# Gates in the output copies, adding gathers and a gate matmul for the last expert, in a two-layer mixture-of-experts step

## The chip, the cores and the metric

One core of a Trainium2 chip runs the whole kernel. The metric is the device time of one execution in microseconds (us), lower is better.

## The reference

One inference step of a decoder with two layers, for 512 prompt rows and 64 sample rows, 1024 columns, all in 32-bit floats. Each layer has a mixer, a residual with layer norm, a mixture of experts and a second residual with layer norm. The change touches the mixture and the norm behind it:

```python
for e in range(N_EXPERTS):                 # 16 experts, D_EXPERT = 256
    he = jax.nn.silu(h @ w_gate[e]) * (h @ w_up[e])
    y = y + gates[:, e:e + 1] * (he @ w_down[e])
x = layernorm(ALPHA * x + y)
```

`gates` has two nonzero entries in each row: the router picks a group of four experts and the two best inside it, and their two scores are normalised to the sum 1. So each row needs two experts only.

## The kernel before

The 576 rows are five tiles, four of 128 and one of 64 (`ROWS`, `NT` = 5). Each engine has its own program; the lines named here are those of the kernel before.

**Jobs and banks.** Each result of TensorE is a numbered job, and job n lives in bank n modulo 8 of the accumulation memory. `claim` waits until the job eight earlier is emptied, `take` waits for the result, `give` marks it emptied, `landed` waits until given jobs are emptied. The numbers are reserved for a version that runs every expert on all rows (288 jobs a layer, used when an expert has more than 128 rows). The usual version (`own_tokens`, line 1195) needs six jobs an expert: T0 and T1 (rows transposed), GU (hidden, 512 columns), HT (hidden transposed), D0 and D1 (the two halves of the output). At its end VectorE increments the semaphores for all the jobs that were left out (lines 2258 to 2265).

**The mixture.** When the router has assigned each row a slot of 128 for each of its two experts, GpSimd scatters the rows into the array `xrows` in main memory (ten indirect transfers, line 983), ScalarE loads 128 rows for each expert (line 1811), and TensorE goes through the experts. In step e it transposes the rows of expert e + 1 (line 1202), transposes the hidden activations of expert e - 1 (line 1222), computes the hidden layer of e (line 1212, 16 passes) and then the output of e - 1 (line 1232, 8 passes). ScalarE copies T0, HT and D0, computes the activation of GU (line 1830); VectorE copies T1 and D1 (line 2257) and computes the product of GU (line 2251). GpSimd stores the copied outputs, 128 rows of 4 KB for each expert, into `yrows` (line 992). SyncE loads the weights of the experts, 3 MB each, into eleven buffers as they come free (lines 958 to 961).

**The end of the mixture.** When all sixteen stores have landed, GpSimd gathers for each tile two rows for each row (ten indirect transfers into `yg`, line 998). VectorE multiplies each by its gate and adds it to `acc`, which ScalarE has filled with ALPHA times x (`combine`, line 2267, two operations at line 2271), then computes the statistics (`row_stats`, 2062: lines 2065, 2067, 2068). ScalarE takes the square root (`norm`, line 1777), VectorE inverts it and makes the offset (`scale_rows`, 2074 and 2075), ScalarE scales the rows (line 1779), VectorE multiplies and adds the norm's parameters (`affine`, 2082 and 2083). The order on VectorE is: scale of tile t, combine and statistics of tile t + 1, affine of tile t.

**Behind it.** After layer 1 each finished tile is stored by GpSimd and the kernel ends. After layer 0 the next mixer begins (`odd`): TensorE transposes each finished tile (`turn_x`, line 1139) and, from the second tile on, computes the latent projection of the tile before (line 1332, 16 passes of 416 columns, one bank). ScalarE's order there is norm of tile t + 1, copy of the transposed tile t (line 1772), copy of the latent projection of tile t - 1 (line 1871). The jobs in order are xT0 (two), xT1 (two), dtok0, xT2 (two), dtok1, and so on; they follow the 288 jobs of the layer. SyncE begins to load the weights of that mixer once all gathers have landed (line 963).

**The start of the kernel.** GpSimd clears `xrows` with one transfer (line 1066) and then stores parts of the pooling state: `pool_p` and `pool_s` in pieces of 60 bytes (512 and 4096 of them), `sgu` in rows. VectorE waits for these three stores before the first mixture.

## Time and profile before

| | |
|---|---|
| Median of 3 runs | 1265.58 us (1265.21 to 1266.97) |
| The profiled execution's own time | 1265.74 us |
| Its span | 1263.9 us |
| Busy TensorE matmul, VectorE, ScalarE, GpSimd | 86%, 41%, 24%, 9% of the span |
| Mixture of layer 0, first row transposes to last output | 228.4 to 414.9 us |
| Mixture of layer 1, the same | 1018.3 to 1204.1 us |

Times in rows are microseconds from the start of the span unless marked ns. PE is TensorE, PEld its weight load, DVE VectorE, ACT ScalarE, POOL GpSimd, SP SyncE. A matmul of 32-bit floats appears as two passes. In the chain of waits each row is the piece of work that released the next one; in the timeline the bracket gives the idle time before an instruction and what ended it.

### The profile page before, as it was taken

The page shows a single profiled execution, that of the slowest core. Times are in us where ns is not written, and L with a number is a line of the kernel's source. Part 1 is how long each engine was busy: PE and PEld are TensorE (multiplying, and loading weights), DVE is VectorE, ACT ScalarE, POOL GpSimd, SP SyncE. Part 2 cuts the span into 40 slices and gives each one's busy share as a digit, 9 for nine tenths or more (in the row PEclk, how much of TensorE's full clock was granted, in tenths as well). Part 3 has the DMA queues.
Part 4 walks back from the last instruction along what each step waited for, and adds up shares of the span by engine and source line. Part 5 has one row for each costly group of instructions (what it writes and reads, how often), then busy time and mean ns, then how long its engine had stood idle before and what let it go on. Part 6 is the DMA issues. An engine that isn't in the chain of part 4 may idle for free.

```text
span 1263.9 us, 19022 instructions
## 1 busy us (share of the span) xinstructions
PE 1089.5 (86%) x7162; PEld 667.3 (53%) x7162; DVE 517.6 (41%) x1330; ACT 302.9 (24%) x691; POOL 112.5 (9%) x152
## 2 busy tenths in 40 slices
PE   7999994799999189999899998999999379999910
PEld 3686452444444056777788875555554244444400
DVE  2570345111111553488545556666334511111155
ACT  0102123111111222323334331455312211111111
POOL 0010003000000300000211111210000300000030
PEclk9999996799999689999999997999999689999965
DMA  9568009899992632132322242854500989999251
GB/s 355 199 244 157 1 5 357 321 364 359 377 352 110 222 128 100 34 100 76 91 74 74 74 133 76 318 191 156 200 34 18 356 314 375 361 367 353 103 199 66
DMA packets 85380, 246.28 MB, mean 195 GB/s; under 512 B 9488, under 2 KB 50496, under 8 KB 66720
## 3 DMA queue, kind: packets, MB, share of 16 engines
q1 hardware_dynamic: 63584, 150.53, 33.9%
q0 software_dynamic: 17088, 77.64, 16.7%
q10 hardware_dynamic: 4608, 16.78, 3.4%
q8 instruction: 62, 1.02, 0.3%
q14 instruction: 38, 0.31, 0.1%
HBM read 205.63 MB, written 58.16 MB: 209 GB/s over the span
## 4 chain that ended last, share of the span: by engine, by line
PE 83%; DVE 8%; issue 4%; DMA 3%; ACT 1%; POOL 1%; POOLq 0%; DVEq 0%; SPq 0%; ACTq 0%
PE bank L1212 18%; PE bank L1148 10%; PE bank L1232 9%; PE bank L1358 8%; PE bank L1282 5%; PE bank L1455 4%; PE bank L1300 3%; PE bank L1202 2%; PE bank L1332 2%; DVE acc L2271 2%; DVE stat L2065 1%; PE bank L1708 1%; PE bank L1733 1%; PE bank L1162 1%; PE bank L1139 1%
## 5 line engine op out<-in xcount | busy, mean ns | idle before, releaser
L1148 PE MATMUL bank<-ring,cat 128*128 128x512 f32 (+1 forms) x320 | 141.0, 594 | 1.3 <-ACT cat L1851 1.3
L1212 PE MATMUL bank<-ring,work 128*128 128x512 f32 x256 | 114.7, 600 | 0.0
L1358 PE MATMUL bank<-xT,ring 128*128 128x288 f32 x448 | 110.9, 407 | 0.0
L2251 DVE TENSOR_TENSOR work<-work,bank 128x256 f32<-128x256 f32 x32 | 13.5, 421 | 219.5 <-ACT work L1830 219.5
L1358 PEld LDWEIGHTS bank<-xT,ring 128*128 128x128 f32 x448 | 84.6, 190 | 24.1 <-issue 1.5
L1148 PEld LDWEIGHTS bank<-ring,cat 128*128 128x128 f32 (+1 forms) x320 | 56.0, 179 | 74.0 <-issue 73.9
L1212 PEld LDWEIGHTS bank<-ring,work 128*128 128x128 f32 x256 | 48.3, 194 | 54.7 <-issue 54.7
L1282 PE MATMUL bank<-xT,ring 128*128 128x288 f32 x256 | 63.1, 407 | 0.0
L1830 ACT ACTIVATE work<-bank 128x256 f32<-128x256 f32 x32 | 12.3, 384 | 208.3 <-PE bank L1212 208.3
L1202 PE MATMUL bank<-const,work 128*128 128x128 f32 x256 | 36.4, 291 | 29.3 <-DMA work<-xrows 29.3
L1232 PE MATMUL bank<-ring,work 128*128 128x512 f32 x128 | 57.7, 593 | 1.0 <-issue 1.0
L2257 DVE COPY work<-bank 128x512 f32<-128x512 f32 x32 | 22.1, 692 | 87.3 <-PE bank L1232 87.3
L1202 PEld LDWEIGHTS bank<-const,work 128*128 128x128 f32 x256 | 32.8, 151 | 44.3 <-DMA work<-xrows 29.6
L1282 PEld LDWEIGHTS bank<-xT,ring 128*128 128x128 f32 x256 | 48.3, 190 | 13.9 <-issue 0.8
L1139 PE MATMUL bank<-const,x 128*128 128x128 f32 (+1 forms) x120 | 17.6, 299 | 38.5 <-DVE x L2083 38.5
L992 POOL DMA_DIRECT2D yrows<-work x32 | 17.2, 538 | 373.9 <-DVE work L2257 370.1
L2090 DVE SCALAR_TENSOR_TENSOR acc<-x,bank 128x512 f32<-128x512 f32 (+1 forms) x20 | 13.7, 685 | 76.3 <-PE bank L1148 76.3
L1300 PE MATMUL bank<-ring,xT 128*128 128x512 f32 (+1 forms) x80 | 37.1, 626 | 7.7 <-DMA ring<-in_stream_dram 7.7
L1212 PE MATMUL bank<-work 128*128 128x512 f32 x96 | 42.5, 592 | 0.0
L1232 PEld LDWEIGHTS bank<-ring,work 128*128 128x128 f32 x128 | 24.2, 190 | 31.1 <-issue 31.1
L1139 PEld LDWEIGHTS bank<-const,x 128*128 128x128 f32 (+1 forms) x120 | 14.6, 163 | 45.7 <-DVE x L2083 41.5
L1820 ACT COPY work<-bank 128x512 f32<-128x512 f32 x32 | 18.7, 586 | 77.7 <-PE bank L1202 77.6
(426 smaller groups left out, 1865.7 us busy)
## 6 DMA issues: line engine op xcount, KB each, us to landing
ring<-in_stream_dram SPq DMA_DIRECT2D x71, 1024.0 KB, 7.4
cat<-in_stream_dram SPq DMA_DIRECT2D x16, 1024.0 KB, 9.0
work<-xrows ACTq DMA_DIRECT2D x32, 512.0 KB, 5.6
xT<-in_stream_dram SPq DMA_DIRECT2D x16, 1024.0 KB, 9.0
work<-in_stream_dram SPq DMA_DIRECT2D x16, 1024.0 KB, 10.5
yrows<-work POOLq DMA_DIRECT2D x32, 512.0 KB, 9.2
by_batch<-in_pages_dram SPq DMA_DIRECT2D x128, 128.0 KB, 2.4
xrows<-work POOLq DMA_DIRECT2D x1, 8192.0 KB, 27.4
```

Of the source, the lines that this page charges most:

```text
L1139: i = pe.transpose(bank(n, 4, P)[:, k, 0:r], x[0:r, tile, P * (4 * g + k):P * (4 * g + k + 1)], ident[0:r, 0:r])
L1148: i = pe.matmul(bank(n)[0:ROWS[tile], :], cat[:, k, tok(tile)], slot(w[k // 4], 4, 512)[:, k % 4, :], start=(k == 0), stop=(k == KC - 1))
L1202: i = pe.transpose(bank(n, 4, P)[:, k, :], xg[:, e % NXG, P * (4 * g + k):P * (4 * g + k + 1)], ident)
L1212: i = pe.matmul(bank(n), xgT[:, e % 2, k, :], sparse_slot(layer, 3 * e + k // 4, 4, 512)[:, k % 4, :], start=(k == 0), stop=(k == KC - 1))
L1232: i = pe.matmul(bank(n), hTS[:, e % 2, k, :], sparse_slot(layer, 3 * e + 2, 2, D_MODEL)[:, k, 512 * half:512 * half + 512], start=(k == 0) ...
L1282: i = pe.matmul(bank(n)[:, 0:nn], slot(w, KC, 256)[:, k, P * (m % 2):P * (m % 2) + P], xT[:, k, a:a + nn], start=(k == 0), stop=(k == KC - 1))
L1300: i = pe.matmul(bank(n)[0:ROWS[tile], :], xT[:, k, tok(tile)], slot(w, 4, 512)[:, k % 4, :], start=(k == 0), stop=(k == KC - 1))
L1332: i = pe.matmul(bank(n)[0:ROWS[tile], 0:D_COLS], xT[:, k, tok(tile)], slot(w[k // 4], 4, 512)[:, k % 4, 0:D_COLS], start=(k == 0), stop=(k ...
L1358: i = pe.matmul(bank(n + s)[:, 0:nn], slot(w, KC, 256)[:, k, P * (m % 2):P * (m % 2) + P], xT[:, k, a:a + nn], start=(k == 0), stop=(k == ...
L1455: i = pe.matmul(bank(n, 4, HD)[rc, j, :], d[a][rc, half, j, :], d[b][rc, half, j, :], start=True, stop=True)
L2257: give(dve.tensor_copy(yS[:, (e - 1) % NYS, 512:], bank(n)), n)
L2271: dve.scalar_tensor_tensor(acc[0:r, tile, :], yg[0:r, tile, k, :], gate2[0:r, tile, k:k + 1], acc[0:r, tile, :], ALU.mult, ALU.add).then_i ...
```

## The change

- `yrows` is stored, already multiplied by the gates. For that each row's two gates are scattered into a new array `grows` (ten indirect transfers of 4 bytes a row, behind the row scatters on GpSimd's queue), and one transfer loads them back as a column for each expert (`gate_of`). ScalarE and VectorE apply them while they copy D0 and D1.
- The gathers write into `acc` and add to it. The second gather of a tile waits for its first; the order is 0, 1, 2, 3 (first rows), 0 (second), 4, then 1, 2, 3, 4 (second).
- The last expert is neither stored nor gathered. Its region of `yrows` is cleared at the start of the kernel. VectorE builds for each tile a matrix with the gate of each row in the column of its slot (`gate_at`), TensorE transposes the five matrices in step 1 (jobs G0 and G1), ScalarE copies the whole last output, and TensorE multiplies the transposed gates with it, two halves a tile, in the last ten of the 288 jobs. VectorE adds these to `acc` after the tile's gathers (`add_last`).
- In step 15 TensorE computes the output of expert 14 before the hidden layer of expert 15, and the copies follow.
- The semaphores of the jobs left out are incremented by SyncE instead of VectorE, and SyncE waits for three tiles' gathers instead of five.
- VectorE's order at the end is: scale of tile t, `add_last` of tile t + 1, affine of tile t, statistics of tile t + 1.
- In `odd` the square root of tile t + 1 comes before the copy of the transposed tile t on ScalarE, the row scaling of tile t + 1 after it.

```diff
@@ -70,7 +70,7 @@
...
 put("ident", np.eye(P))
-put("lane", i % D_ROPE * 1.0)
+put("lastslots", np.tile((N_EXP - 1) * P + np.arange(P) * 1.0, (P, 1)))
 put("cum", np.concatenate([chunk & (i <= t), chunk & (i < t)], 1))
@@ -282,18 +282,28 @@
-SPARSE = ["T0", "T1", "GU", "HT", "D0", "D1"]
+LAST_E = N_EXP - 1
 SPARSE_ORDER = {}
...
 for e in range(N_EXP + 1):
-    for at, kind in ((e + 1, "T0"), (e + 1, "T1"), (e - 1, "HT"), (e, "GU"), (e - 1, "D0"), (e - 1, "D1")):
+    steps = [(e + 1, "T0"), (e + 1, "T1")] + ([(LAST_E, "G0"), (LAST_E, "G1")] if e == 1 else []) + [(e - 1, "HT")]
+    outputs = [(e - 1, "D0"), (e - 1, "D1")]
+    for at, kind in steps + (outputs + [(e, "GU")] if e == LAST_E else [(e, "GU")] + outputs):
         if 0 <= at < N_EXP:
             SPARSE_ORDER[at, kind] = len(SPARSE_ORDER)
+DENSE = N_EXP * (8 + 2 * NT)
 def sparse_job(layer, e, kind):
     return job(f"{layer}.e0") + SPARSE_ORDER[e, kind]
+def last_job_of(layer, tile, half):
+    return job(f"{layer}.e0") + DENSE - 2 * NT + 2 * tile + half
 def rec(name, tile, half=0):
@@ -551,13 +561,15 @@
+last_gates = sem("last_gates")
+gates_scattered = sem("gates_scattered")
+gates_loaded = sem("gates_loaded")
-combined = [sem(f"combined{k}") for k in range(LAYERS)]
@@ -742,10 +753,15 @@
...
 spare = [t[:, SLOT * i:SLOT * i + SLOT] for t in (cat_t, xT_t, work) for i in range(2)]
+tail_t = sb("tail", P + NS)
+gate_at = [view(cat_t, 4 * D_MODEL + P * tile, P) for tile in range(NT - 1)] + [view(tail_t, 0, P)]
+gate_by = [view(work, 4 * D_MODEL + P * tile, P) for tile in range(NT - 1)] + [view(tail_t, P, NS)]
 zero = work[:, WORK - D_MODEL - 16:WORK - 16]
...
 xrows = nc.dram_tensor("xrows", [(N_EXP - 1) * P + P * NT, D_MODEL], F32).ap()
+grows = nc.dram_tensor("grows", [(N_EXP - 1) * P + P * NT, 1], F32).ap()
+gate_of = view(stat, 400, N_EXP)
 yrows = nc.dram_tensor("yrows", [N_EXP * P, D_MODEL], F32).ap()
@@ -959,7 +975,17 @@
...
     load_spare(layer, j)
-for tile in range(NT):
+first = job(f"{layer}.e0")
+used = len(SPARSE_ORDER)
+landed(sp, first + used - NBANK, NBANK)
+for b in range(NBANK):
+    skipped = sum(1 for m in range(first + used, first + DENSE - 2 * NT) if m % NBANK == b)
+    sp.sem_inc(filled[b], skipped)
+    sp.sem_inc(emptied[b], skipped)
+at = FIRST_EXPERT_BLOCK[layer]
+for i in range(NSLOT):
+    sp.sem_inc(slot_loaded[i], 16 * sum(1 for j in range(NSLOT, 3 * N_EXP) if (at + j) % NSLOT == i))
+for tile in range(3):
     sp.wait_ge(gathered[layer][tile], 32)
@@ -973,7 +999,7 @@
...
 def pool_mixture(layer):
-    pool.wait_ge(rows_cleared, 16)
+    pool.wait_ge(rows_cleared, 48)
     pool.wait_ge(early_rows, layer + 1)
@@ -983,22 +1009,39 @@
...
                 in_=x[0:r, tile, :], in_offset=None).then_inc(scattered[layer], 16)
+    for tile in range(NT):
+        r = ROWS[tile]
+        for k in range(2):
+            pool.indirect_dma_start(
+                out=grows, out_offset=bass.IndirectOffsetOnAxis(ap=rowi[0:r, 2 * tile + k:2 * tile + k + 1], axis=0),
+                in_=gate2[0:r, tile, k:k + 1], in_offset=None).then_inc(gates_scattered, 16)
     flag = is_crowded(pool, layer)
...
     with pool.Else():
-        for e in range(N_EXP):
+        pool.wait_ge(gates_scattered, 32 * NT * (layer + 1))
+        pool.dma_start(gate_of, grows[0:N_EXP * P].rearrange("(e p) o -> p (e o)", p=P), allow_slow_non_contiguous=True)\
+            .then_inc(gates_loaded, 16)
+        for e in range(LAST_E):
             landed(pool, ejob(layer, e, "D0"), 2)
...
         for i in range(NYS):
-            pool.wait_ge(y_stored[layer][i], 16 * ((N_EXP - 1 - i) // NYS + 1))
-        for tile in range(NT):
+            pool.wait_ge(y_stored[layer][i], 16 * ((LAST_E - 1 - i) // NYS + 1))
+        pool.wait_ge(acc_scaled, NT * (layer + 1))
+        def add_rows(tile, k):
             r = ROWS[tile]
-            for k in range(2):
-                pool.indirect_dma_start(
-                    out=yg[0:r, tile, k, :], out_offset=None, in_=yrows,
-                    in_offset=bass.IndirectOffsetOnAxis(ap=rowi[0:r, 2 * tile + k:2 * tile + k + 1], axis=0))\
-                    .then_inc(gathered[layer][tile], 16)
+            pool.indirect_dma_start(
+                out=acc[0:r, tile, :], out_offset=None, in_=yrows,
+                in_offset=bass.IndirectOffsetOnAxis(ap=rowi[0:r, 2 * tile + k:2 * tile + k + 1], axis=0),
+                compute_op=ALU.add).then_inc(gathered[layer][tile], 16)
+        for at in range(NT + 3):
+            if at < NT:
+                add_rows(at, 0)
+            if at >= 3:
+                pool.wait_ge(gathered[layer][at - 3], 16)
+                add_rows(at - 3, 1)
 def recurrence():
@@ -1065,6 +1108,8 @@
...
     .then_inc(rows_cleared, 16)
+pool.dma_start(grows[0:N_EXP * P].rearrange("(p e) o -> p (e o)", p=P), zero[:, 0:N_EXP]).then_inc(rows_cleared, 16)
+pool.dma_start(yrows[LAST_E * P:N_EXP * P, :], zero).then_inc(rows_cleared, 16)
 store(pool, outs["pool_p"].rearrange("p (g r) -> p g r", g=HB), aP[:, :, 16 + SEQ - POOL_BUF:])
@@ -1234,16 +1279,43 @@
...
             done(i, n)
+    def turn_gates():
+        pe.wait_ge(last_gates, layer + 1)
+        for g, tiles in enumerate((range(NT - 1), (NT - 1,))):
+            n = ejob(layer, LAST_E, f"G{g}")
+            claim(pe, n)
+            for tile in tiles:
+                r = ROWS[tile]
+                i = pe.transpose(bank(n)[:, P * tile if g == 0 else 0:][:, 0:r], gate_at[tile][0:r],
+                                 ident[0:r, 0:r])
+            done(i, n)
+    def last_output(tile):
+        r = ROWS[tile]
+        for half in range(2):
+            n = last_job_of(layer, tile, half)
+            claim(pe, n)
+            done(pe.matmul(bank(n)[0:r, :], gate_by[tile], yS[:, LAST_E % NYS, 512 * half:512 * half + 512],
+                           start=True, stop=True), n)
     turn_rows(0)
...
             turn_rows(e + 1)
+        if e == 1:
+            turn_gates()
         if e > 0:
             turn_hidden(e - 1)
+        if e == LAST_E:
+            output(e - 1)
         if e < N_EXP:
             hidden(e)
-        if e > 0:
+        if e > 0 and e != LAST_E:
             output(e - 1)
+    landed(pe, ejob(layer, LAST_E, "G0"), 2)
+    landed(pe, ejob(layer, LAST_E, "D0"), 2)
+    for tile in range(NT):
+        last_output(tile)
 def every_expert(layer):
@@ -1771,13 +1843,20 @@
...
         give(act.copy(xT[:, 4 * g:4 * g + 4, tok(tile)], bank(n, 4, P)[:, :, 0:ROWS[tile]]), n)
-def norm(k, tile):
+def norm_root(k, tile):
+    r = ROWS[tile]
+    act.wait_ge(ln_var, NT * k + tile + 1)
+    act.activation(rstd[0:r, tile:tile + 1], rstd[0:r, tile:tile + 1], ACT.Sqrt).then_inc(ln_std, 1)
+def norm_rows(k, tile):
     i, r = NT * k + tile, ROWS[tile]
-    act.wait_ge(ln_var, i + 1)
-    act.activation(rstd[0:r, tile:tile + 1], rstd[0:r, tile:tile + 1], ACT.Sqrt).then_inc(ln_std, 1)
     act.wait_ge(ln_affine, i + 1)
...
                    scale=rstd[0:r, tile:tile + 1]).then_inc(ln_scaled, 1)
+def norm(k, tile):
+    norm_root(k, tile)
+    norm_rows(k, tile)
 def router_scores(layer, batch):
@@ -1810,6 +1889,17 @@
...
     act.dma_start(xg[:, e % NXG, :], xrows[P * e:P * e + P, :]).then_inc(xg_loaded[layer][e % NXG], 16)
+def copy_output(e):
+    if e >= NYS:
+        act.wait_ge(y_stored[layer][e % NYS], 16 * (e // NYS))
+    for half in range(2 if e == LAST_E else 1):
+        n = ejob(layer, e, f"D{half}")
+        if e == 0:
+            act.wait_ge(gates_loaded, 16 * (layer + 1))
+        take(act, n)
+        give(act.activation(yS[:, e % NYS, 512 * half:512 * half + 512], bank(n), ACT.Copy,
+                            scale=1.0 if e == LAST_E else gate_of[:, e:e + 1]), n)
 act.wait_ge(scattered[layer], 32 * NT)
@@ -1818,10 +1908,16 @@
...
     give(act.copy(xgT[:, (e + 1) % 2, 0:4, :], bank(n, 4, P)), n)
+if e == 1:
+    n = ejob(layer, LAST_E, "G0")
+    take(act, n)
+    give(act.copy(work[:, 4 * D_MODEL:4 * D_MODEL + 4 * P], bank(n)), n)
 if e > 0:
...
     give(act.copy(hTS[:, (e - 1) % 2, :, :], bank(n, 2, P)), n)
+if e == LAST_E:
+    copy_output(e - 1)
 if 0 <= e < N_EXP:
@@ -1831,12 +1927,8 @@
...
                     load_rows(e + NXG)
-            if e > 0:
-                n = ejob(layer, e - 1, "D0")
-                if e - 1 >= NYS:
-                    act.wait_ge(y_stored[layer][(e - 1) % NYS], 16 * ((e - 1) // NYS))
-                take(act, n)
-                give(act.copy(yS[:, (e - 1) % NYS, 0:512], bank(n)), n)
+            if e > 0 and e != LAST_E:
+                copy_output(e - 1)
 def gate(m):
@@ -1874,8 +1966,10 @@
...
 if tile + 1 < NT:
-    norm(1, tile + 1)
+    norm_root(1, tile + 1)
 copy_xT(f"xT{tile}", tile)
+if tile + 1 < NT:
+    norm_rows(1, tile + 1)
 if tile > 0:
@@ -2240,45 +2334,57 @@
...
 with dve.Else():
-    for e in range(-1, N_EXP + 1):
+    def copy_output(e):
+        n = ejob(layer, e, "D1")
+        if e >= NYS:
+            dve.wait_ge(y_stored[layer][e % NYS], 16 * (e // NYS))
+        if e == 0:
+            dve.wait_ge(gates_loaded, 16 * (layer + 1))
+        take(dve, n)
+        give(dve.tensor_scalar(yS[:, e % NYS, 512:], bank(n), gate_of[:, e:e + 1], None, ALU.mult), n)
+    for tile in range(NT):
+        r = ROWS[tile]
+        i = dve.tensor_scalar(gate_at[tile][0:r], c("lastslots", r), t0[0:r, tile, LAST_E:], gates[0:r, tile, LAST_E:],
+                              ALU.is_equal, ALU.mult)
+    i.then_inc(last_gates, 1)
+    for e in range(-1, N_EXP):
         if e + 1 < N_EXP:
...
             give(dve.tensor_copy(xgT[:, (e + 1) % 2, 4:8, :], bank(n, 4, P)), n)
-        if 0 <= e < N_EXP:
+        if e == 1:
+            n = ejob(layer, LAST_E, "G1")
+            take(dve, n)
+            give(dve.tensor_copy(gate_by[NT - 1], bank(n)[:, 0:NS]), n)
+        if e == LAST_E:
+            copy_output(e - 1)
+        if e >= 0:
             n = ejob(layer, e, "GU")
...
             give(dve.tensor_tensor(hS[:, e % 2, :], hgS, bank(n)[:, D_EXP:], ALU.mult), n)
-        if e > 0:
-            n = ejob(layer, e - 1, "D1")
-            if e - 1 >= NYS:
-                dve.wait_ge(y_stored[layer][(e - 1) % NYS], 16 * ((e - 1) // NYS))
-            take(dve, n)
-            give(dve.tensor_copy(yS[:, (e - 1) % NYS, 512:], bank(n)), n)
-    landed(dve, ejob(layer, N_EXP - 1, "D1") - NBANK + 1, NBANK)
-    skipped = (N_EXP * (8 + 2 * NT) - N_EXP * len(SPARSE)) // NBANK
-    for b in range(NBANK):
-        dve.sem_inc(filled[b], skipped)
-        dve.sem_inc(emptied[b], skipped)
-    for s in range(NSLOT):
-        first = FIRST_EXPERT_BLOCK[layer]
-        dve.sem_inc(slot_loaded[s], 16 * sum(1 for j in range(NSLOT, 3 * N_EXP) if (first + j) % NSLOT == s))
-    def combine(tile):
+        if 0 < e < LAST_E:
+            copy_output(e - 1)
+    def add_last(tile):
         r = ROWS[tile]
         dve.wait_ge(gathered[layer][tile], 32)
-        for k in range(2):
-            dve.scalar_tensor_tensor(acc[0:r, tile, :], yg[0:r, tile, k, :], gate2[0:r, tile, k:k + 1],
-                                     acc[0:r, tile, :], ALU.mult, ALU.add).then_inc(combined[layer], 1)
-            dve.wait_ge(combined[layer], 2 * tile + k + 1)
-        row_stats(2 * layer + 1, tile)
-    combine(0)
+        for half in range(2):
+            n = last_job_of(layer, tile, half)
+            cols = slice(512 * half, 512 * half + 512)
+            take(dve, n)
+            give(dve.tensor_tensor(acc[0:r, tile, cols], bank(n)[0:r, :], acc[0:r, tile, cols], ALU.add), n)
+        landed(dve, last_job_of(layer, tile, 0), 2)
+    add_last(0)
+    row_stats(2 * layer + 1, 0)
     for tile in range(NT):
...
         if tile + 1 < NT:
-            combine(tile + 1)
+            add_last(tile + 1)
         affine(2 * layer + 1, tile)
+        if tile + 1 < NT:
+            row_stats(2 * layer + 1, tile + 1)
 assert step.count[0] == steps_after
```

## Rows read from the trace of the kernel before

**Rows 1.** The page, part 4: the chain that ended last, shares by engine

```profile
PE 83%; DVE 8%; issue 4%; DMA 3%; ACT 1%; POOL 1%; POOLq 0%; DVEq 0%; SPq 0%; ACTq 0%
```

**Rows 2.** The chain of waits, end of layer 1: start us, us, what

```profile
1189.38 6.87 PE bank L1212 x16
...
1199.90 0.51 issue
...
1200.41 3.69 PE bank L1232 x8
...
1209.86 5.21 DMA work<-yrows,rowi
...
1215.09 1.30 DVE acc L2271
```

**Rows 3.** Timeline, end of layer 1: start us, us, engine line op, tiles

```profile
1196.70 0.42 DVE L2251 TENSOR_TENSOR work<-work,bank 128x256 f32<-128x256 f32 x1 [6.74 <-ACT work L1830]
...
1208.57 0.99 POOL L998 DMA_INDIRECT work<-yrows,rowi  x1 [2.62 <-DMA yrows<-work]
...
1217.73 1.29 DVE L2065 BATCH_NORM_STATS2 stat<-acc 128x6 f32<-128x512 f32 x2
...
1219.72 0.16 DVE L2074 RECIPROCAL stat<-stat 128x1 f32<-128x1 f32 x1 [0.27 <-ACT stat L1777]
...
1220.03 0.89 POOL L998 DMA_INDIRECT work<-yrows,rowi  x1 [0.30 <-issue]
...
1220.11 1.24 ACT L1779 ACTIVATE x<-acc,stat 128x1024 f32<-128x1024 f32 x1 [0.42 <-DVE stat L2075]
...
1225.55 1.23 DVE L2083 TENSOR_TENSOR x<-x,lnp 128x1024 f32<-128x1024 f32 x1
...
1250.47 1.22 DVE L2083 TENSOR_TENSOR x<-x,lnp 64x1024 f32<-64x1024 f32 x1
```

**Rows 4.** The page, part 5: VectorE adding from a bank

```profile
L2090 DVE SCALAR_TENSOR_TENSOR acc<-x,bank 128x512 f32<-128x512 f32 (+1 forms) x20 | 13.7, 685 | 76.3 <-PE bank L1148 76.3
```

**Rows 5.** DMA from 1208 to 1226 us, then the stores of line 992

```profile
GB/s 0 0 0 0 0 118 109 355 401 273 291 319 337 410 391 328 300 246 300 291 337 346 364 373 410 373 410 419 437 401 419 437 410 237 200 164 137 100 27 18
...
work<-yrows,rowi POOLq DMA_INDIRECT x10, 6.1
...
DMA to landing us min/median/max: 2.9/9.2/10.9
```

**Rows 6.** Timeline of TensorE, end of layer 0

```profile
444.58 1.97 PE L1139 MATMUL bank<-const,x 128*128 128x128 f32 x8 [4.98 <-DVE x L2083]
...
446.34 7.30 PE L1332 MATMUL bank<-ring,xT 128*128 128x416 f32 x16
...
453.47 1.04 PE L1139 MATMUL bank<-const,x 128*128 128x128 f32 x8
...
461.37 1.09 PE L1139 MATMUL bank<-const,x 128*128 128x128 f32 x8 [1.28 <-DVE x L2083]
...
468.63 11.59 PE L1332 MATMUL bank<-ring,xT 128*128 128x416 f32 x32
```

**Rows 7.** Clearing and stores at the start, then scatter and copy in layer 0

```profile
xrows<-work POOLq DMA_DIRECT2D x1, 8192.0 KB, 27.4
...
77.25 1.18 POOL L1066 DMA_DIRECT2D xrows<-work  x1 [58.47 <-DVE work L2304]
...
79.05 1.82 POOL L896 DMA_DIRECT2D out_pool_s_dram<-work  x1
...
DMA to landing us min/median/max: 39.1/39.1/39.1
...
124.72 0.69 DVE L2090 SCALAR_TENSOR_TENSOR acc<-x,bank 128x512 f32<-128x512 f32 x1 [3.78 <-PE bank L1148]
...
220.66 0.90 POOL L983 DMA_INDIRECT xrows<-x,rowi  x1 [0.30 <-issue]
...
250.18 0.58 ACT L1839 COPY work<-bank 128x512 f32<-128x512 f32 x1 [1.33 <-PE bank L1232]
```

1 line of the change is left out of this document (removed).

## The prediction, made before the changed kernel ran

> **What bounds the kernel now.** I read the chain that ended last first: TensorE is 83% of the span and VectorE 8% [rows 1], and one expert after the other runs without a gap in its matmuls, so inside the expert loop only TensorE work counts. Then I read the chain and the timeline where the loop ends, since the change sits there. Both layers end alike. In layer 1 the second-last expert's hidden activations are transposed by 1189.38, when the last expert's hidden matmuls begin, and its output matmuls end at 1204.10 (1200.41 + 3.69), the last store leads to the first gather at 1208.57, and the second gather (it is half of tile 0) releases VectorE at 1215.09 [rows 2, 3]. From there VectorE sets the end: 36.6 us to the end of its last operation at 1251.69 [rows 3]. So two tails of a transfer chain plus a VectorE chain are what can be won. In layer 0 the tail feeds TensorE again; there the profile of TensorE says what follows [rows 6].
>
> **The stores and gathers start earlier.** The second-last expert's outputs are now computed ahead of the last expert's hidden layer, and the last expert is no longer stored. Added ahead of it: turning the gates, 5 transposes. Eight cost 1.04 us at full clock [rows 6], so 0.65 us. The transpose of hidden rows then ends at 1190.0. The output matmuls follow at once, so they have to wait for ScalarE's copy; the same sequence at the old end shows 0.51 of wait and 3.69 of matmuls [rows 2], giving 1194.2. Old: end of matmuls 1204.10 to first gather 1208.57 is 4.47 us (copy, issue, landing; unloaded stores land in 2.9 us [rows 5]). New first gather: 1198.7, which is 9.9 us earlier.
>
> **The gathers themselves.** They now add to the residual. Plain ones move 400 to 437 GB/s once running [rows 5], 1.25 us for the 512 KB of a tile, as fast as GpSimd issues them (10 from 1208.57 to 1220.03 [rows 3]). No row shows one that adds. From below: it costs as much as a plain one, 1.25 us. From above: reading the row, reading the residual and writing the sum don't overlap at all, 3.75 us. I take 2.5 us: twice the bytes are read, the write runs beside it as it does today. The order is 0,1,2,3 (first rows), 0 (second), 4, 1, 2, 3, 4, tile 4 being half a tile. Data begins 1.7 us after the first issue (about 1210.3 in the rates of [rows 5]) and the last byte is reported about 1.1 us after it moved. Tile 0 is complete after five transfers: 1198.7 + 1.7 + 5 x 2.5 + 1.1 = 1214.0, 1.1 us ahead of the old 1215.09. The Trainium skill (Collectives: The Full Stack, "The bandwidth ceiling") says that an adding transfer needs two source reads and runs at half the rate of a copy, the addition itself being free; by that the sum is the same, and no run here shows it yet.
>
> **The last expert by matmul.** Its outputs are copied whole by ScalarE and multiplied by the transposed gates, two matmuls a tile. TensorE comes there late: 1194.2 + 6.87 hidden [rows 2] + 0.95 waiting for ScalarE's activation and VectorE's product, which today other matmuls cover (the product is 0.42 [rows 3]) + 0.26 for two transposes + 0.51 + 3.69 = 1206.5, against 1204.10 today. The copy ends about 1207.1, the SyncE bookkeeping of the skipped banks costs at most about a microsecond (no row; an estimate), and a tile's two matmuls take 1.8 (3.69 for the four of an output). VectorE could add tile 0 from about 1208.5 to 1209.5. The gathers at 1214.0 hide all of this; without that cover 4 to 5 us would be the limit of the gain.
>
> **The VectorE chain.** Per tile today: 2.60 combining (2 x 1.30 [rows 2]), 1.29 + 0.47 statistics, 0.36 scale, 2.46 affine (two of 1.22), 6.95 with gaps. New: 2 adds from a bank, 0.685 each [rows 4], 1.4 together, but the statistics follow the affine, so ScalarE's square root stands open, 0.25. Period 1.4 + 2.46 + 1.76 + 0.25 + 0.36 = 6.25. First affine done at start + 7.75 (1.45 + 1.76 + 0.23 + 0.36 + 1.45 + 2.5), where it was + 11.7 (1225.55 + 1.23 less 1215.09 [rows 2, 3]). The end: 7.75 + 4 x 6.25 - 0.15 = 32.6 instead of 36.6, **4.0 us** less. Tile 1's rows are complete at 1198.7 + 1.7 + 6.5 x 2.5 + 1.1 = 1217.75, and VectorE wants them at 1214.0 + 3.85 = 1217.85; later tiles have more room.
>
> **Layer 1's tail: 1.1 + 4.0 = 5.1 us gained.** The output store behind it stays.
>
> **Layer 0's tail.** The start gains the same 1.1, the first affine comes 3.95 earlier relative to it. The second affine comes 6.95 after the first, as today: the split of the norm lets ScalarE copy tile 0 first, and its row scaling (1.24 [rows 3]) comes behind that copy, which costs what the shorter adds win. TensorE's second turn, today at 444.58 [rows 6], comes 5.05 earlier. Behind it a new wait: the first latent matmuls use a bank that now holds the last expert's contribution to tile 3, and this is added only after the second affine. Today they start 1.8 us after that turn began [rows 6]; new about 3.1. Their 7.30 end at + 10.4. Then the turn of tile 2 needs the bank of tile 4's first half, whose addition waits for the square root behind ScalarE's latent copy: free at + 12.0, turned at + 12.6, where today it is turned at + 9.95 [rows 6]. From there to the end of the latent matmuls today takes 480.2 - 454.5 = 25.7, of which the 1.28 us wait before tile 3's turn (461.37) [rows 6] falls away: + 12.6 + 24.4 = + 37.0, where today it is 480.2 - 444.6 = 35.6. **1.4 us given back.** The weights for these matmuls are asked for once all gathers are in; new, once three tiles are, so they come no later against their use. Layer 0: 1.1 + 3.95 - 1.4 = 3.65 us gained.
>
> **The gates' own transfers.** Ten scatters of 4-byte pieces behind the row scatters on GpSimd (the last of these at 220.66 in layer 0 [rows 7]) at 1.25 us each end at 234.2. Landed under load by 243 (stores land in 9.2 us at the median [rows 5]). Then one load of 2048 pieces. The nearest row is the old store of 4096 pieces of 60 bytes: queued behind the clearing (77.25 + 27.4 = 104.7), landed at 79.05 + 39.1 = 118.2, at most 13.5 us [rows 7]. Half of that plus a loaded landing is 16: ready at 259 at worst, 250 likely. The first gated copy is due at 250.18 on ScalarE [rows 7] (ahead of it nothing new but one 0.58 copy); behind it on that engine stand the copies of expert 3's rows and of the next hidden transpose, and TensorE misses the latter only from about 262. Cost zero, with 3 us to spare at worst. The Trainium skill (DMA: Bandwidth & Descriptors, "Rules for kernel authors") has one descriptor for each element of such a strided load. By that it is 2048 of them, and the sum stays. In the prologue the clearing of the last expert's rows adds 512 KB, 1.7 us at the rate of the 8192 KB one [rows 7]; VectorE, which waits for stores behind it, then waits 3.78 us for TensorE [rows 7]: hidden. The 5 gate products of VectorE lie in its wait for the first rows, which land after the last scatter [rows 7]; gated copies cost what plain ones do.
>
> **Sum.** 3.65 + 5.1 = 8.75. The profiled execution took 1265.74 (span 1263.9 and 1.8 around it), 0.16 above the median of 1265.58. 1265.74 - 8.75 = **1257.0 us**.
>
> **Rivals.** (a) The adding gathers run at the plain rate: tile 0 is then complete at 1198.7 + 4 x 1.25 for the issue of four + 1.0 for the wait on the first and the next issue + 5.2 to landing (that of the second gather today [rows 2]) = 1209.9, 5.2 earlier than before. Gain 5.2 x 2 + 3.95 + 4.0 - 1.4 = 16.95: **1248.8**. For: the write side is no busier, and the addition costs VectorE nothing; against: twice the reads. (b) **Slower: the adding gathers cost 3.75 us**, read, read, write in turn. Tile 0 at 1220.25, 5.15 late, tile 1 another 1.8: layer 1 loses 5.15 + 1.8 - 4.0 = 2.95, layer 0 4.4: **1273.1**. It decides from 3.2 us a gather on; each tenth costs 1 us over both layers. For: five of ten stand in one queue ahead of the first use; against: today's gathers keep 16 DMA engines streaming. (c) Slower: the gates' load comes later than 262, because each 4-byte piece takes a turn behind a weight packet. A loaded store is 6.3 us slower for its 8 rows per DMA engine [rows 5]; 128 pieces each at that price would be 100 us. But TensorE's stall stops new weight loads, so the queue empties: I price it at 8 us a layer, 16 - 8.75 slower, **1273**. (d) The bank wait in layer 0 and TensorE's late end cost more, or the earlier start is eaten by slower issue: **1264**, no change.
>
> **Numbers.** (main) 0.44, (a) 0.20, (b) 0.18, (c) 0.06, (d) 0.12. Faster by over 0.2% (2.5 us, about what a measurement of this kernel can tell) needs a gather under 3.0 us: the main case, (a) and a little of the others, 0.67. Same 0.13, slower 0.20. Range 1248 to 1270: it takes in (a) and leaves out the worst of (b) and (c); the main case alone, at 2.2 to 2.9 us a gather, is 1254 to 1261.
>
> **What would show it.** The first gather near 1198.7 less what layer 0 gained, landings (6.1 at the median today) of 7 to 12 us; VectorE's first addition of the last expert about 15 us after that gather, released by a gather, not by TensorE; 32.6 us from there to VectorE's end; in layer 0 a TensorE wait for VectorE before the second and third turns; in the first two experts no ScalarE wait for the gates. Wrong would be: TensorE idle in the second expert, or VectorE released by TensorE in the tail.

## The result and the profile after

The changed kernel takes **1269.59 us** (median of 6 runs, 1268.42 to 1271.14), the one before 1265.28 beside it: ratio 1.0036, 95% interval 1.0024 to 1.0047. It is slower by 0.36%, where 1257.0 was forecast. The time of one and the same kernel varies from execution to execution: of the 69 of the kernel before timed beside the experiments, 53 have a mean granted clock of 0.930 to 0.935 and a median of 1264.9 us, and 16 one of 0.927 to 0.929 and 1268.3 us. The profiled execution took 1268.42 with a span of 1266.6, against 1265.74 and 1263.9 before, so the traces, of one execution of each kernel, show 2.7 of the 4.3 us.

The page of the changed kernel, top: busy time, share of the span and instructions. Against before, VectorE has less to do (it was 41%) and GpSimd more (it was 9%), as the change intends.

```profile
span 1266.6 us, 19184 instructions
...
PE 1113.2 (88%) x7212; PEld 677.7 (54%) x7212; DVE 508.7 (40%) x1340; ACT 307.9 (24%) x695; POOL 145.2 (11%) x174
```

The timeline of GpSimd at the end of layer 1 answers to the gathers of [rows 3]. Seen: 1.84 us from one issue to the next (1.25 before), and the last one waits 3.23 us for a landing.

```profile
1205.30 1.67 POOL L1034 DMA_INDIRECT acc<-yrows,rowi  x1 [3.23 <-DMA yrows<-work]
...
1212.84 1.54 POOL L1034 DMA_INDIRECT acc<-yrows,rowi  x1 [0.30 <-issue]
...
1225.29 1.43 POOL L1034 DMA_INDIRECT acc<-yrows,rowi  x1 [3.23 <-DMA acc<-yrows,rowi]
```

The DMA view of the changed kernel, 1205 to 1232 us in 40 slices, answers to the rates of [rows 5]: about 200 GB/s where plain gathers move 400.

```profile
GB/s 0 0 0 24 133 127 158 194 194 158 194 206 206 170 188 212 194 200 194 218 212 231 206 200 182 200 188 182 200 194 206 225 206 206 225 194 206 225 194 79
...
acc<-yrows,rowi POOLq DMA_INDIRECT x10, 9.8
```

The timeline of VectorE, end of layer 1, answers to [rows 2, 3]: its first addition waits 15.48 us for a gather, and from there it takes 32.5 us to the end of its last operation (1254.67 + 1.22).

```profile
1223.36 1.29 DVE L2376 TENSOR_TENSOR acc<-bank,acc 128x512 f32<-128x512 f32 x2 [15.48 <-DMA acc<-yrows,rowi]
...
1227.52 1.29 DVE L2376 TENSOR_TENSOR acc<-bank,acc 128x512 f32<-128x512 f32 x2 [0.42 <-DMA acc<-yrows,rowi]
...
1254.67 1.22 DVE L2177 TENSOR_TENSOR x<-x,lnp 64x1024 f32<-64x1024 f32 x1
```

The timeline of TensorE, end of layer 1: the two waits, 0.93 and 0.51, before the last output and 0.96 for SyncE's bookkeeping, then the contributions of tiles 0 to 3, done at 1220.6 us, 2.7 before VectorE adds the first of them.

```profile
1207.94 0.44 PE L1267 MATMUL bank<-const,work 128*128 128x128 f32 x2 [0.93 <-DVE work L2365]
1208.89 3.67 PE L1277 MATMUL bank<-ring,work 128*128 128x512 f32 x8 [0.51 <-issue]
1213.52 7.11 PE L1298 MATMUL bank<-work 128*128 128x512 f32 x16 [0.96 <-SPq L984]
```

**Where the time went** is read from the timelines of both, cut at the same pieces of work. Columns: the kernel before, the changed one, and six of the experiments described below. Each column is one execution; where no instruction of a stage differs, the columns still differ by up to 0.7 us, and by 1.2 in the first row (25.3, 26.5 and 26.3 with an unchanged layer 0).

| Stage, us | before | changed | only layer 1 | only layer 0 | code shifted | changed, shifted | scatters alone | early sum, shifted |
|---|---|---|---|---|---|---|---|---|
| last router transposes to first row transposes, layer 0 | 25.3 | 27.6 | 26.5 | 27.5 | 26.3 | 27.9 | 27.6 | 26.1 |
| to the last output of layer 0 | 186.5 | 187.3 | 186.2 | 187.5 | 185.7 | 187.6 | 185.3 | 188.8 |
| to the end of the latent matmuls | 65.3 | 64.0 | 65.4 | 63.9 | 65.0 | 65.4 | 64.8 | 58.7 |
| **to the last router transposes of layer 1** | **511.4** | **515.6** | 511.1 | **515.9** | **517.9** | 511.2 | 510.9 | 512.0 |
| to the first row transposes of layer 1 | 26.6 | 28.4 | 28.2 | 26.4 | 26.2 | 28.6 | 28.1 | 25.8 |
| to the last output of layer 1 | 185.8 | 187.4 | 187.4 | 185.9 | 186.0 | 188.9 | 185.0 | 188.7 |
| to VectorE's first statistics | 13.6 | 12.2 | 12.5 | 13.7 | 13.7 | 10.8 | 13.9 | 7.2 |
| to VectorE's end | 34.0 | 31.1 | 31.3 | 34.0 | 34.0 | 32.1 | 33.9 | 32.1 |
| to the end of the span | 12.2 | 10.7 | 11.0 | 11.3 | 12.2 | 10.8 | 11.0 | 12.1 |

One stage stands out. Between the latent matmuls of layer 0 and the router of layer 1 the diff changes no instruction, and yet this stage is 4.1 us longer (515.56 against 511.42). The last row's 1.5 us is no gain of the change: with the end of the kernel unchanged it reads 11.0 to 12.2.

The two kernels can be laid over each other there, instruction by instruction. From 628 to 740 us the changed one stands 1.88 us behind, constantly. Then comes a wait. The timeline of TensorE, kernel before:

```profile
740.90 1.97 PE L1524 MATMUL bank<-ring 64*64 64x128 f32 x64
743.79 0.33 PE L1540 MATMUL bank<-const,xT 64*64 64x64 f32 x4 [0.93 <-issue]
...
747.86 2.02 PE L1455 MATMUL bank<-ring 64*64 64x64 f32 x31
```

and the changed kernel, the same work:

```profile
742.77 1.97 PE L1596 MATMUL bank<-ring 64*64 64x128 f32 x64
746.71 0.33 PE L1612 MATMUL bank<-const,xT 64*64 64x64 f32 x4 [1.98 <-ACT xT L2070]
...
752.40 3.57 PE L1527 MATMUL bank<-ring 64*64 64x64 f32 x31
```

A wait of 0.93 has become 1.98, and behind it the same 31 matmuls take 3.57 instead of 2.02. The windows view says why (us, busy time of PE, PEld, DVE, ACT and POOL with their counts, granted clock, DMA share, GB/s). Before:

```profile
729.00:743.00 14.00, 12.72 (x287) 11.25 (x283) 12.87 (x33) 3.51 (x10) 3.60 (x5) 1.00 0.61 204
743.00:757.00 14.00, 13.21 (x194) 10.38 (x195) 3.70 (x8) 5.51 (x14) 0.00 (x0) 1.00 0.28 80
```

Changed:

```profile
731.00:745.00 14.00, 12.60 (x283) 11.13 (x279) 12.74 (x33) 3.64 (x10) 3.60 (x5) 1.00 0.58 197
745.00:759.00 14.00, 12.29 (x120) 9.26 (x121) 1.68 (x4) 3.77 (x10) 0.00 (x0) 0.63 0.28 78
```

The granted clock is 0.63 in a stretch where it was 1.00. By 757 us the changed kernel stands 7.3 us behind instead of 1.9; later it wins 2 back, since before the clock falls too: from 1.00 up to 762.6 us to 0.50 from 765 us, behind a wait of TensorE for VectorE, 1.98 us, which the changed kernel has as well. A smaller part of the 4.1, 0.8 us, is lost at 620 us: there both kernels wait 2.79 us for VectorE, and the granted clock from 612 to 626 us is 0.88 before and 0.76 changed. Why that differs was not followed up. Why TensorE waits 1.05 us longer at this one place is what the experiments had to find.

### The profile page after: what moved, and what is told of

Read it like the earlier page. It is cut to its first block, busy times and chain, and to the rows that moved or that the text cites. A ratio compares the mean times of both kernels' runs of the same rounds, so it can differ in the third digit from the quotient of the medians.

```text
span 1266.6 us, 19184 instructions
## 1 busy us (share of the span) xinstructions
PE 1113.2 (88%) x7212; PEld 677.7 (54%) x7212; DVE 508.7 (40%) x1340; ACT 307.9 (24%) x695; POOL 145.2 (11%) x174
## 4 chain that ended last, share of the span: by engine, by line
PE 53%; DVE 4%; issue 3%; DMA 2%; ACT 1%; POOL 1%; DVEq 0%; POOLq 0%; ACTq 0%
PE bank L1430 8%; PE bank L1257 8%; PE bank L1193 5%; PE bank L1277 4%; PE bank L1527 4%; PE bank L1404 2%; PE bank L1247 1%; PE bank L1780 1%; PE bank L1805 1%; PE bank L1507 1%; PE bank L1544 1%; PE bank L1739 1%; DMA acc<-yrows,rowi 1%; PE bank L1756 1%; PE bank L1554 1%
## 5 line engine op out<-in xcount | busy, mean ns | idle before, releaser
L1247 PEld LDWEIGHTS bank<-const,work 128*128 128x128 f32 x256 | 32.5, 151 | 48.3 <-DMA work<-xrows 33.6
L2344 DVE TENSOR_SCALAR work<-bank,stat 128x512 f32<-128x512 f32 x30 | 22.5, 751 | 81.7 <-PE bank L1277 81.7
L2184 DVE SCALAR_TENSOR_TENSOR acc<-x,bank 128x512 f32<-128x512 f32 (+1 forms) x20 | 13.7, 685 | 74.6 <-PE bank L1193 74.6
L1527 PE MATMUL bank<-ring 64*64 64x64 f32 x944 | 35.6, 222 | 1.3 <-DVE ring L2652 1.1
## 6 DMA issues: line engine op xcount, KB each, us to landing
work<-xrows ACTq DMA_DIRECT2D x32, 512.0 KB, 5.5
yrows<-work POOLq DMA_DIRECT2D x31, 512.0 KB, 9.1
xrows<-work POOLq DMA_DIRECT2D x1, 8192.0 KB, 25.3
```

Of the source, the lines that this page charges most:

```text
L1247: i = pe.transpose(bank(n, 4, P)[:, k, :], xg[:, e % NXG, P * (4 * g + k):P * (4 * g + k + 1)], ident)
L1527: i = pe.matmul(bank(n, 4, HD)[rc, j, :], d[a][rc, half, j, :], d[b][rc, half, j, :], start=True, stop=True)
L2344: give(dve.tensor_scalar(yS[:, e % NYS, 512:], bank(n), gate_of[:, e:e + 1], None, ALU.mult), n)
```

## The experiments

All medians of before in these runs lie between 1264.9 and 1265.8.

### 1. The adding gathers' price

The changed kernel with plain gathers, so that each row of the residual is overwritten instead of summed:

```diff
                 out=acc[0:r, tile, :], out_offset=None, in_=yrows,
...
-                compute_op=ALU.add).then_inc(gathered[layer][tile], 16)
+                ).then_inc(gathered[layer][tile], 16)
```

> The changed kernel with gathers that write instead of adding. It leaves out the sum into the residual. Theory 1 (the adding gathers are what made the tails late: 1.85 us to issue and about 200 GB/s against 1.25 us and 400 GB/s before): issue falls back to 1.25 us, tile 0 is complete 11 to 12 us after the first gather instead of 17.5 and 18.1, each tail gets 5.5 to 6.5 us shorter and the time is 11 to 13 us below the changed kernel, 1257 to 1259. Rival (issue order and the wait for a tile's first gather are the limit, not the addition): less than 3 us a tail, time above 1263.

1258.22 us, ratio 0.994 (0.9917 to 0.9964). The timeline of VectorE and then the DMA view from 1199 to 1217 us of this kernel:

```profile
1212.32 1.29 DVE L2375 TENSOR_TENSOR acc<-bank,acc 128x512 f32<-128x512 f32 x2 [9.57 <-DMA acc<-yrows,rowi]
```

```profile
GB/s 0 0 0 0 0 0 109 118 291 428 264 155 155 273 382 391 382 373 291 282 364 382 382 391 373 391 155 173 255 182 291 401 410 428 428 346 437 410 228 100
```

Tile 0 is free 12.2 us after the first gather's issue (1200.16) instead of 18.1, the stage up to the first statistics is 5.9 us shorter in layer 1 and 5.3 in layer 0. So adding in the transfer costs some 11 us in all, which is the kernel's difference from the changed one (1258.22 against 1269.59). The addition itself is left out here, not moved to an engine. The stage between the mixtures still takes 515.7: the slow gathers have nothing to do with it, and neither has the moment at which it begins, since this kernel enters it 4.2 us earlier than before.

### 2. The gates' transfers

The changed kernel without the ten scatters and the load of the gates; the gated outputs are then multiplied by zero.

```diff
-                        pool.indirect_dma_start(
-                            out=grows, out_offset=bass.IndirectOffsetOnAxis(ap=rowi[0:r, 2 * tile + k:2 * tile + k + 1], axis=0),
-                            in_=gate2[0:r, tile, k:k + 1], in_offset=None).then_inc(gates_scattered, 16)
...
-                    pool.wait_ge(gates_scattered, 32 * NT * (layer + 1))
...
-                                act.wait_ge(gates_loaded, 16 * (layer + 1))
...
-                            dve.wait_ge(gates_loaded, 16 * (layer + 1))
```

> The changed kernel without the ten gate scatters and the gate load of each layer. It leaves out the gates: the experts' outputs are multiplied by 0. Theory 1 (the small scatters, queued behind the row scatters, hold up the first loads of rows): the four row loads land in 3.2 us again instead of 5.3 and 5.5, each mixture starts about 2 us earlier, the time falls by 3 to 4 us. Rival (the loads are late for another reason): the first row load still takes over 5 us and the time stays within 1 us of 1269.6.

1267.85 us, ratio 1.0018 (1.0002 to 1.0034), and the stage before layer 1's mixture is 26.2 instead of 28.4, as expected. But the mixtures behind are 1.4 (layer 0) and 1.1 us longer than in the changed kernel, and the time is 1.7 us below the changed kernel's, not 3 to 4; the two intervals overlap. The stage between the mixtures: 515.9.

Then the other way round: before, with the ten scatters and nothing that reads them.

> The kernel before, with the ten scatters of the gates added behind the row scatters in each layer, and nothing that reads them. Theory A: they stand in the queues between the row scatters and the first row loads and make the start of each mixture 1.8 to 2 us longer (from 26.6 to 28.4 us in layer 1): 1265.3 + 3.7 = 1269. Theory B: the start is longer because of the gate products on VectorE and the transposes of the gates: no change here, 1265.3.

1266.64 us, ratio 1.0004 (0.9989 to 1.0019). Both theories were half right. The start is longer by 1.5 us in layer 1 and 2.3 in layer 0, as theory A has it, but the mixtures behind are 0.8 and 1.2 shorter, and no loss can be measured in the whole, as theory B has it. The 2.3 is the upper end: layer 0 without these scatters reads 25.3 to 26.7 us in this stage over all traces, and with them 27.5 to 27.9. The chain of waits before the first row transposes of layer 1 shows the place; kernel before:

```profile
1009.12 5.96 DMA xrows<-x,rowi
...
1015.10 3.15 DMA work<-xrows
```

Changed:

```profile
1014.34 5.34 DMA xrows<-x,rowi
...
1019.70 5.47 DMA work<-xrows
```

The load of the first rows lands after 5.47 instead of 3.15 us: it stands behind the scatters' 4-byte pieces. The timelines of the other kernels agree: from the issue of this load to TensorE's first transposes it takes 3.2 to 3.3 us in every layer without the scatters and 4.8 to 5.9 in every layer with them.

### 3. The split norm

Before, with the order of ScalarE's square root, copy and row scaling in layer 0's tail as in the change.

> The kernel before with only the split of the square root and the row scaling around the copy of the transposed tile in the second layer's start. Theory 1: the copy of tile 0 comes about 1 us earlier and the scaling 1 us later, TensorE's second turn moves by less than 1 us, the time stays within 1 us of 1265.3. Rival (the stage between layer 0's latent matmuls and layer 1's router, 511.4 us before and 515.6 us changed, depends on when it begins): a shift of under 1 us changes that stage by 2 us or more through TensorE's granted clock.

1264.93, ratio 0.9995 (0.9978 to 1.0011). No difference can be measured, and the stage between the mixtures takes 510.9.

### 4. Each layer alone

The whole change in one layer, the other as before (`yrows` is then one array for each layer).

> The kernel before, with the whole change in layer 1 alone (layer 0, its tail and its norm as before). My theory: the change itself loses about 2 us at the start of a mixture (the gates' scatters delay the first row loads), 1.6 us by the late end of TensorE, and wins about 1.4 us up to the first statistics, 2.9 us in VectorE's chain and 1.5 us behind it; the rest of the loss of the changed kernel stands between the mixtures, where after a changed layer 0 the recurrence takes 515.6 us instead of 511.4. Then this kernel takes 1265.3 - 2.4 = about 1263, and the stretch from the end of layer 0's latent matmuls to the last transposes before layer 1's mixture takes 511 to 512 us. Rival 1: the recurrence's longer time comes with the kernel's code or memory as a whole: the stretch is 515 us here too and the time 1267. Rival 2: layer 1 suffered from what happened before it; undisturbed it gives the 5.1 us I forecast for it: 1260.

> The kernel before, with the whole change in layer 0 alone. My theory: layer 0 loses 2 us at its start, and at the end of its latent matmuls it stands about 1 us later than before; the recurrence behind it loses 4 us by TensorE's clock; layer 1 is as before: 1265.3 + 1 + 4 = 1270.5. Rival: the two halves of the loss are evenly spread, each layer costs 2.1 us: 1267.4, and the recurrence takes 511.4 us.

Layer 1 alone: **1262.88** (1259.86 to 1266.49, 12 runs), ratio 0.9977 (0.9966 to 0.9988): faster. Layer 0 alone: **1269.5** (1267.47 to 1271.74, 7 runs), ratio 1.0031 (1.0018 to 1.0045), about the whole loss. The stage between the mixtures is 511.1 in the first and 515.9 in the second. So it is something in layer 0, which comes ahead of that stage.

### 5. The place of the code

Before, with waits on a semaphore long reached, on TensorE alone, where it idles 22 us:

```diff
                     if e > 0:
                         output(e - 1)
+                if layer == 0:
+                    for i in range(106):
+                        pe.wait_ge(scattered[0], 16 + 16 * (i & 1))
```

> The kernel before with 106 waits on a semaphore that has long been reached (53 instructions of TensorE), in layer 0 behind the last expert's output, where TensorE waits 22 us for the first tile: no work is added, but all later TensorE code lies 53 instructions further on, as many as the change adds there. Theory A, the place of the code: TensorE's code arrives late at another place of the recurrence, at 744 us TensorE stands idle for 2 us instead of 1, the granted clock falls, the recurrence takes 514 to 516 us instead of 511.4 and the kernel 1268 to 1270. Theory B, the recurrence is slow behind the change because of the moment at which it starts, or because of what the other engines do: no change, 511.4 and 1265.

**1270.85** (1268.43 to 1271.97, 7 runs), ratio 1.0038 (1.0024 to 1.0052). The waits themselves cost nothing where they stand (stages 2 and 3 of the table are no longer than before), and nothing else is changed, but the stage between the mixtures takes 517.9. The timeline of TensorE of this kernel, the same work as above:

```profile
740.20 1.97 PE L1527 MATMUL bank<-ring 64*64 64x128 f32 x63
744.18 0.27 PE L1527 MATMUL bank<-ring 64*64 64x128 f32 x1 [2.01 <-issue]
...
750.38 3.57 PE L1458 MATMUL bank<-ring 64*64 64x64 f32 x31
```

Here the wait can't be put down to any engine: TensorE stands still for 2.01 us between the 63rd and the 64th of one group of equal matmuls that wait for nothing. Then come the same 3.57 us, and the windows view of this kernel has the same granted clock, 0.62:

```profile
742.00:756.00 14.00, 11.99 (x121) 8.72 (x115) 1.43 (x4) 3.77 (x9) 0.00 (x0) 0.62 0.32 90
```

Theory B is out. All seven executions of this kernel have a mean granted clock of 0.927 to 0.929, as 16 of the 69 of the kernel before have without any shift. So the kernel before can lose these microseconds by itself at times; whether at this same place, its one trace (0.930) can't show.

The converse: the changed kernel, with 170 such waits (85 instructions) behind the last expert's contributions in layer 0.

> The changed kernel with 170 waits on a semaphore that has long been reached (85 instructions of TensorE) in layer 0 behind the last expert's contributions, where TensorE waits for the first tile. With the 53 instructions of the change this puts the recurrence's code 138 instructions behind its place in the kernel before, where the version with the diagonal matmuls had it and the recurrence took 511.9 us. Theory A (place of the code): TensorE's 2 us idle at 744 us is gone or short, the recurrence takes 511 to 513 us instead of 515.6, and the kernel takes 1269.6 - 3.5 = 1266. Theory B (something else of the change disturbs the recurrence): 515.6 us and 1269.6.

1268.27 (1265.68 to 1271.67, 12 runs), ratio 1.0017 (1.0003 to 1.0032). The stage is back at 511.2, with a wait of 0.93 at that place, and behind it the windows view of this kernel has the full clock:

```profile
747.00:761.00 14.00, 13.69 (x199) 10.87 (x200) 3.71 (x8) 5.58 (x13) 0.00 (x0) 1.00 0.26 73
```

The time fell by only 1.3 us, and its interval overlaps with the changed kernel's, so the converse is shown by the stage and not by the whole time. One reason is in the trace: here the waits were not free, which I had taken them to be. The timeline of TensorE, end of layer 0:

```profile
430.01 1.93 PE L1298 MATMUL bank<-work,tail 128*64 128x512 f32 x4 [3.08 <-DVE acc L2379]
440.40 1.94 PE L1184 MATMUL bank<-const,x 128*128 128x128 f32 x8 [8.46 <-issue]
```

They stand behind tile 4's contribution, which itself waits for a bank, and take 8.46 us; the first tile was ready at 437.63, the end of its affine in VectorE's timeline, 2.8 us earlier. The mixture of layer 1 was 1.5 us longer as well, and that is not explained.

### 6. A version without adding gathers and gate transfers

Plain gathers of the first fifteen experts' rows into free memory beside the last expert. VectorE makes diagonal matrices of the gates, and TensorE sums everything in the bank:

```diff
+    pe.matmul(bank(n)[0:r, :], gate_by[tile], yS[:, LAST_E % NYS, cols], start=True, stop=False)
+    for k in range(2):
+        i = pe.matmul(bank(n)[0:r, :], diag_of[tile][k][0:r, 0:r], got[tile][k][0:r, cols],
+                      start=False, stop=(k == 1))
```

> A version without gate transfers and without adding gathers: ungated outputs are stored, plain gathers start after expert 14's store and land in the idle buffers of x, cat and xT, and TensorE sums both gathered rows (times a diagonal matrix of the gates) and the last expert's rows in one bank, from which VectorE adds to the residual. Theory 1: row loads land in 3.2 us, the first gather is as early as in the changed kernel, tile 0 is limited by TensorE (six matmuls, 5.2 us, from about 4 us after the last output), VectorE's statistics of tile 0 begin 3 us earlier than in the kernel before and its chain is 3 us shorter: 6 us less in layer 1, 3 to 5 in layer 0, 1254 to 1257. Rival: TensorE's matmuls run at the half clock in that stretch, 10 us a tile pair, and the tail is no shorter than before: above 1262.

1268.11, ratio 1.0029 (1.0012 to 1.0047): a miss. In layer 1 the stage to the first statistics fell to 7.2 us. The stage between the mixtures is 511.9, with the code 138 TensorE instructions further on. In layer 0 the end of the latents came 7.7 us later than before. The timeline of VectorE of this kernel shows a wait of its own making: ScalarE scales tile 1 behind the copy of transposed tile 0, and TensorE turns tile 0 only behind all thirty of these matmuls.

```profile
447.54 1.23 DVE L2164 TENSOR_TENSOR x<-x,lnp 128x1024 f32<-128x1024 f32 x1 [12.22 <-ACT x L1844]
```

So the diagonals go into layer 1 alone, with layer 0 as before:

> Layer 0 as before. In layer 1 the early plain gathers and the diagonal gate matmuls of the version before this one: ungated outputs are stored, the rows of fifteen experts are gathered beside the last expert, TensorE sums gate times row and the last expert's rows in one bank, VectorE adds the bank. No gate scatters, no adding gathers. My theory, from that version's layer 1: outputs end 2.4 to 2.8 us later, first statistics 6.4 us earlier relative to that (7.2 instead of 13.6), VectorE's chain 1.9 us shorter: 1265.3 - 5.7 = about 1259.5, recurrence 511.4. Rival: the recurrence is disturbed here as well (515), 1263.

**1259.63** (1257.97 to 1262.59), ratio 0.9958 (0.9943 to 0.9973), as worked out from the first version's rows.

In layer 0 VectorE, which is idle while the last expert runs, multiplies and adds the early rows, and ScalarE copies the last expert's rows out of the banks, so that TensorE's turns don't wait for them:

> Layer 1 with the diagonal matmuls as in the version that took 1259.6. In layer 0 the rows of fifteen experts are gathered plainly beside the last expert, VectorE multiplies and adds them (two operations a tile as before) as soon as they are there, TensorE brings the last expert's rows with the gate product, and ScalarE copies those of tiles 1 to 4 out of the banks. From the rows: last outputs at 416.5, tile 0's sum at about 421.4 instead of 427.2 and its affine at about 430 instead of 437.6, period 8.4 us a tile on VectorE: the layer's latents end 4 us earlier, at 476. Rest as in that version: 1255.5. But by the theory of the place of the code, its 53 added TensorE instructions in layer 0 bring the recurrence to 515.6 us instead of 510.8: then 1260.

> The kernel before this one with 170 waits on a reached semaphore (85 instructions of TensorE) in layer 0 where TensorE waits, so that the recurrence's code stands 138 instructions behind its place in the kernel before. Theory A: recurrence 511 to 513 us and 4 us less than the same kernel without the shift, about 1256. Theory B: no difference from it.

1259.16 (1255.13 to 1261.93), ratio 0.9936 (0.9916 to 0.9956), and shifted **1256.65** (1255.46 to 1260.31, 6 runs), ratio 0.992 (0.9901 to 0.9938), faster than both kernels. The stage between the mixtures takes 514.7 and 512.0. The unshifted version again has 53 more TensorE instructions ahead and shows the wait of 1.98 at the same matmuls. The timeline of TensorE of this version:

```profile
740.82 0.33 PE L1606 MATMUL bank<-const,xT 64*64 64x64 f32 x4 [1.98 <-ACT xT L2069]
```

With the shift by 138 TensorE does not wait less there, but in two pieces. The timeline of the shifted version, then its windows view:

```profile
740.97 1.52 PE L1593 MATMUL bank<-ring 64*64 64x128 f32 x43 [1.46 <-issue]
...
743.28 0.33 PE L1609 MATMUL bank<-const,xT 64*64 64x64 f32 x4 [0.78 <-issue]
...
747.29 2.02 PE L1524 MATMUL bank<-ring 64*64 64x64 f32 x31
```

```profile
729.00:743.00 14.00, 10.90 (x250) 10.01 (x245) 11.05 (x27) 3.50 (x12) 2.20 (x3) 1.00 0.64 205
743.00:757.00 14.00, 13.72 (x199) 10.90 (x200) 3.71 (x8) 5.54 (x13) 0.00 (x0) 1.00 0.24 70
```

1.46 and 0.78 are 2.24 us, more than the 1.98 of the other kernels, and still the granted clock stays at 1.00 and the 31 matmuls take 2.02. So in these traces the fall comes behind one unbroken wait of 2 us, and not behind two waits that together are longer.

The medians of the two versions differ by 2.5 us, the stages by 2.8; the intervals of the ratios overlap.

## Why the prediction was wrong

The forecast was a gain of 8.75 us: 3.65 in layer 0, 5.1 in layer 1. The trace shows a loss of 2.7: layer 0 ends 1.1 later, the stage behind it takes 4.1 more, and layer 1 wins 2.5, of which 1.5 are the last row of the table. Three steps of the prediction failed: it put the work between the mixtures at no change, the adding gathers at 15.3 us to tile 0 where they took 17.5 and 18.1, and the gates' transfers at nothing.

**Nothing between the mixtures was costed.** This is the largest single loss; without its 4.1 us the traces would differ by 1.4 us the other way, about the size of the table's last row. The sum took it that work which the diff leaves alone keeps its time. The 53 added TensorE instructions of layer 0 move all later code, TensorE then stands still 2 us instead of 1 at one place, the clock falls, and 3 to 6.5 us are gone. Shown by the table and the stages given with the experiments: every kernel that adds 53 instructions ahead (the changed one and its variants of experiments 1 and 2, layer 0 alone, the shifted one, the early sum) has 514.7 to 517.9, and every kernel with 0 or 138 has 510.8 to 512.0. Only these three places were tried, each kernel with one trace, so nothing here forecasts what another shift would do. That the missing thing is the code itself, loaded late, fits the idle time between two equal matmuls; no row shows the loading as its cause, and that stays argued.

**A gather: 2.5 us, measured 2.8, and more of them ahead.** In layer 1 186 GB/s are moved from 1207.3 to 1223.3, which makes 2.8 us of 512 KB. The first byte comes 2.0 us after the issue (1.7 forecast). And tile 0 is not done after five transfers: 16.0 us of data at 2.8 are 5.7 transfers, or 5.3 if the forecast's own 1.1 us from the last byte to its report is taken off, so bytes of the transfers issued behind it had moved too. Together 18.1 us from first issue to VectorE's first addition, and 17.5 in layer 0, against 15.3. That is 2.8 and 2.2 us lost, some 1.6 of each by the price of a gather. So the term was mis-sized and its mechanism right: the gather's price lies in the main case (2.2 to 2.9 us), for which 1254 to 1261 was forecast, rival (a) at the plain rate is what experiment 1 shows with the addition left out, and rival (b) at 3.75 is out. The Trainium skill (Collectives: The Full Stack, "The bandwidth ceiling") puts the adding phase of a collective at half the rate of the copying one. This case's gathers come near that: about 200 GB/s against 400 once running, and 186 on the mean against 300 of the plain gathers, each from the first byte to VectorE's first addition (1202.1 to 1212.3 in experiment 1).

**"Cost zero" for the gates' own transfers.** The gates were in time, as argued: their load was issued at 242.30 and landed in 8.4 to 8.9 us, and ScalarE waited 1.4 us for it once. But I asked only whether they come in time, not what they delay. They stand between the row scatters and the first row load, which took 5.47 us instead of 3.15: the start is 1.8 us longer in layer 1 and up to 2.3 in layer 0, of which the scatters-alone kernel of experiment 2 got 0.8 to 1.2 back in the mixture.

**Layer 0's tail.** Tile 1's gathers were to be on time; VectorE waits 1.35 us for them, so the first affine ends 8.95 us after the start instead of 7.75. The bank wait behind the second turn was right (2.95 us against 3.1), and from there to the latents' end it took 38.2 instead of 37.0, with the first latent matmuls at 8.39 instead of 7.30 us at a lower granted clock (0.69 against 0.80 from 446.2 to 454.4 us). The timeline of TensorE:

```profile
436.54 1.97 PE L1184 MATMUL bank<-const,x 128*128 128x128 f32 x8 [6.33 <-DVE x L2177]
443.12 1.97 PE L1184 MATMUL bank<-const,x 128*128 128x128 f32 x8 [4.61 <-DVE x L2177]
```

**Right:** VectorE's chain (32.5 against 32.6; the first affine ended 0.3 us later than forecast, and a period is 6.14 instead of 6.25 us; the parts given for today's period add up to 7.18, not to the 6.95 that the rows show), the first gather 180.1 us after the first row transposes of layer 1 (180.4 by 1198.7 less 1018.3), TensorE's late end hidden by the gathers, VectorE released by a gather and not by TensorE. The 0.20 for slower was made of a gather at 3.75 us and of gates that come too late. Neither happened; the largest loss came from a place that no rival had. The measured 1269.59 lies inside the stated range, 0.4 us from its end, and that is luck: the range reached so far for those two rivals.

## What to carry to other kernels

Adding in the transfer takes the addition off the engines but not off the queues: where a gather's end is waited for, it cost 11 us here, and the version with plain gathers and the sums on VectorE and TensorE, at the same place of the code, took 1259.2 against 1269.6. Small transfers that nobody waits for yet still stand ahead of the next load that somebody waits for. And where a change adds instructions to a kernel whose granted clock falls and rises, time the same number of instructions without their work, in a place where the engine idles, before the difference is put down to the idea.
